# Sparse attention: an instruction order by groups of two key blocks in place of whole steps

## The reference, cut to what matters

```python
def selected_attention(q, k, v, pos, sel, slopes):      # 16 heads of 64, two key groups
    ...
        s = jnp.einsum('bghqd,bgqnld->bghqnl', qc, kg).astype(jnp.float32) * DK ** -0.5
        s = s - slopes[None, :, :, None, None, None] * dist[:, :, None]
        s = jnp.where(valid[:, :, None], s, NEG_INF).reshape(B, G, HPG, Q_BLOCK, n_top * SLC_BLOCK)
        p = jax.nn.softmax(s, axis=-1).reshape(B, G, HPG, Q_BLOCK, n_top, SLC_BLOCK).astype(v.dtype)
        return jnp.einsum('bghqnl,bgqnld->bghqd', p, vg)
...
def window_attention(q, k, v, pos, slopes):             # the same over the last 256 keys
    ...
        p = jax.nn.softmax(jnp.where(valid, s, NEG_INF), axis=-1).astype(v.dtype)
        return jnp.einsum('bghqk,bgkd->bghqd', p, vb)
...
    g = jax.nn.sigmoid(gates).reshape(B, S, 3, G, HPG).transpose(2, 0, 3, 4, 1)[..., None]
    o = g[0] * o_cmp + g[1] * o_slc + g[2] * o_win
```

## Time and profile before

| | |
|---|---|
| median of three runs | 2252.74 us |
| lowest, highest | 2248.02, 2253.5 us |
| the profiled execution: span from first to last instruction | 2245.4 us |
| the three runs less that span | 2.6 to 8.1 us, 7.3 at the median |
| mean granted TensorE clock over the span | 0.944 |
| TensorE busy in the span | 1981.3 us (88%) |
| VectorE, ScalarE, GpSimd busy | 947.7, 698.9, 456.3 us |
| sparse attention, first scores to last add | 1341.5 to 1731.5 us |
| PE busy in 1341 to 1732 | 352.87 of 391 us |

### The profile page before, as it was taken

One profiled execution on the slowest core, in us unless ns is written; L12 is line 12 of the kernel. 1 busy time (PEld: TensorE's weight loads), 2 busy tenths in 40 slices (PEclk: granted clock), 3 DMA queues, 4 the chain that ended last, 5 costly groups with the idle time before them and its releaser, 6 DMA issues. The chain is left out here.

```text
span 2245.4 us, 30273 instructions
## 1 busy us (share of the span) xinstructions
PE 1981.3 (88%) x11225; PEld 1262.1 (56%) x11225; DVE 947.7 (42%) x2302; ACT 698.9 (31%) x1761; POOL 456.3 (20%) x617
## 2 busy tenths in 40 slices
PE   6998859999969989859999768999999996999997
PEld 3444436655556756545655435666666555756664
DVE  3896874533252112114223486666664225211111
ACT  4013555531101111112122566667665110111111
POOL 0001003321022212110000255454544002122111
PEclk9999969999979999989999979999999997999999
DMA  5000010121387999863000200001001117799993
GB/s 216 0 0 0 0 47 20 39 88 66 153 362 285 383 348 377 314 210 70 1 0 1 78 1 11 11 11 48 20 11 34 77 72 316 256 379 364 353 340 119
DMA packets 80888, 307.77 MB, mean 137 GB/s; under 512 B 18352, under 2 KB 23495, under 8 KB 63846
## 3 DMA queue, kind: packets, MB, share of 16 engines
q1 hardware_dynamic: 66342, 272.23, 31.2%
q0 software_dynamic: 14400, 33.59, 5.9%
HBM read 276.75 MB, written 47.89 MB: 145 GB/s over the span
## 5 line engine op out<-in xcount | busy, mean ns | idle before, releaser
L1110 POOL TENSOR_SCALAR nsaatt_probs<-nsaatt_probs,nsaatt_inv,trunk_gates_or_logits 128x384 f32<-128x384 f32 (+7 forms) x256 | 185.6, 739 | 200.7 <-DVE nsaatt_inv L1137 200.7
L1123 DVE CUSTOM_DVE_ANT_0 nsaatt_probs<-nsaatt_scores,trunk_arena 128x384 f32<-128x384 f32 (+7 forms) x256 | 151.3, 629 | 86.3 <-PE nsaatt_scores L1029 85.7
L1834 DVE TENSOR_TENSOR experts_sig<-experts_gu_ps,experts_sig 128x256 f32<-128x256 f32 x50 | 21.2, 424 | 388.0 <-ACT experts_sig L1799 388.0
L1081 ACT ACTIVATE nsaatt_probs<-nsaatt_probs,nsaatt_bias 128x384 f32<-128x384 f32 (+7 forms) x256 | 169.0, 667 | 8.7 <-DVE nsaatt_bias L1132 8.6
L1039 PE MATMUL nsaatt_turn<-trunk_ident,nsaatt_probs 128*128 128x128 f32 x912 | 123.8, 279 | 23.4 <-POOL nsaatt_probs L1110 6.0
L1029 PE MATMUL nsaatt_scores<-layer_k_cols,trunk_x_rows 64*128 64x384 f32 (+3 forms) x640 | 128.9, 513 | 14.6 <-DVE nsaatt_top L1123 13.4
L1701 PEld LDWEIGHTS experts_gu_ps<-experts_x_cols,moew_w 128*128 128x128 f32 x1152 | 134.0, 197 | 12.1 <-issue 12.1
L1701 PE MATMUL experts_gu_ps<-experts_x_cols,moew_w 128*128 128x128 f32 x1152 | 136.7, 281 | 4.6 <-DVE experts_x_cols L1787 4.6
L1799 ACT ACTIVATE experts_sig<-experts_gu_ps 128x256 f32<-128x256 f32 x50 | 19.2, 383 | 381.0 <-PE experts_gu_ps L1701 243.6
L1039 PEld LDWEIGHTS nsaatt_turn<-trunk_ident,nsaatt_probs 128*128 128x128 f32 x912 | 97.3, 140 | 57.5 <-issue 37.6
L1713 PE MATMUL experts_gu_ps<-moew_w,experts_x_cols 128*64 128x512 f32 x256 | 97.0, 667 | 23.9 <-issue 23.9
(11 more groups left out here) (425 smaller groups left out, 3737.4 us busy)
## 6 DMA issues: line engine op xcount, KB each, us to landing
moew_w<-in_moe_w_gate_dram SPq DMA_DIRECT2D x34, 1024.0 KB, 12.4
moew_w<-in_moe_w_up_dram SPq DMA_DIRECT2D x34, 1024.0 KB, 18.2
moew_w<-in_moe_w_down_dram SPq DMA_DIRECT2D x34, 1024.0 KB, 25.6
trunk_arena<-in_moe_w_gate_dram SPq DMA_DIRECT2D x20, 1024.0 KB, 12.3
trunk_arena<-in_moe_w_up_dram SPq DMA_DIRECT2D x20, 1024.0 KB, 16.8
trunk_arena<-in_moe_w_down_dram SPq DMA_DIRECT2D x20, 1024.0 KB, 24.2
trunk_x_rows<-in_moe_w_gate_dram SPq DMA_DIRECT2D x10, 1024.0 KB, 16.3
trunk_x_rows<-in_moe_w_up_dram SPq DMA_DIRECT2D x10, 1024.0 KB, 22.3
```

The lines of the kernel that those rows point to most:

```text
L1081: act.activation(part(s, r, h), part(s, r, h), ACT.Exp, bias=bias[:, b, i:i + 1], scale=steps[s]["scale"][h], accum_out=total[:, b, i:i + ...
L1110: pool.tensor_scalar(part(s, r, h), part(s, r, h), inv[:, s % BUFS, i:i + 1], 1.0 if gate is None else gate[h], ALU.mult, ALU.mult).then_i ...
L1123: dve.tensor_tensor_reduce(part(s, r, h), scores_of(s, r, h), br["mask"], 1.0, -3e38, ALU.add, ALU.max, top[:, s % BUFS, i:i + 1]).then_in ...
```

## The change

In layer 1 (BR is 2) the loops over whole steps give way to one loop over the group number n. At position n TensorE does the values of group n-3, then the transposes of group n, then those scores that are due. The other engines run through the same positions with their own part. What is due is set by five constants: a branch's scores, masks, exponentials and inverses are placed 13, 12, 9 and 4 (window: 5) units ahead of its first group, where a group of two blocks counts 3/2.7 and one of a single block 2/2.7. The add of a step stands at the position of its last value. Layer 0's order stays, and so do all instructions, waits, tiles and buffers.

```diff
+SCORE_LAG = 13
+MASK_LAG = 12
+EXP_LAG = 9
+INV_LAG = 4
+VALUE_LAG = 3
...
+    opens = [n for n, g in enumerate(flat) if g[2] == 0]
+    weight = np.cumsum([0] + [(hi - lo + 1) / 2.7 for s, r, lo, hi in flat])
+    ENDS = range(-2 * SCORE_LAG, len(flat) + VALUE_LAG + 1)
+
+    def slot(u, lag):
+        at = weight[opens[u]] - lag
+        return int(np.floor(at)) if at < 0 else int(np.searchsorted(weight, at + 1e-9, side="right")) - 1
...
 TensorE
-                for s in range(S):
-                    if s + AHEAD < S:
-                        score(s + AHEAD, 0)
-                        if BR > 1 and not wide(s + AHEAD):
-                            score(s + AHEAD, 1)
-                    for n in range(first[s], first[s + 1]):
-                        value(n)
-                    if s + AHEAD < S and wide(s + AHEAD):
-                        score(s + AHEAD, 1)
-                    if s + 1 < S:
-                        for n in range(first[s + 1], first[s + 2]):
+                    u = 0
+                    for n in ENDS:
+                        if 0 <= n - VALUE_LAG < len(flat):
+                            value(n - VALUE_LAG)
+                        if 0 <= n < len(flat):
                             turn(n)
+                        while u < S * BR and slot(u, SCORE_LAG) <= n:
+                            score(u // BR, u % BR)
+                            u += 1
...
 ScalarE
+                    i = 0
+                    for n in ENDS:
+                        if 0 <= n < len(flat) and by_act[n]:
+                            copy_group(act, copy, n, copied_act)
+                        while i < S * SUB and slot(i // 2, EXP_LAG) + i % 2 <= n:
+                            exps(i // SUB, i % SUB // 2, i % 2)
+                            i += 1
...
 VectorE
+                    u = v = s = 0
+                    for n in ENDS:
+                        while v < S * BR and slot(v, INV_LAG + v % BR) <= n:
+                            inverse(v // BR, v % BR)
+                            v += 1
+                        if s < S and first[s + 1] - 1 + VALUE_LAG <= n:
+                            add(s)
+                            s += 1
+                        while u < S * BR and slot(u, MASK_LAG) <= n:
+                            mask(u // BR, 2 * (u % BR))
+                            mask(u // BR, 2 * (u % BR) + 1)
+                            biased(u // BR, u % BR)
+                            u += 1
+                        if 0 <= n < len(flat) and not by_act[n]:
+                            copy_group(dve, dve.tensor_copy, n, copied_dve)
```

More of the change, by code:

```diff
@@ L1055, in value @@
                     last.then_inc(valued, 1)
[L1057 to L1061, removed]
-                for s in range(S):
-                    if s + AHEAD < S:
-                        score(s + AHEAD, 0)
-                        if BR > 1 and not wide(s + AHEAD):
-                            score(s + AHEAD, 1)
-                    for n in range(first[s], first[s + 1]):
-                        value(n)
-                    if s + AHEAD < S and wide(s + AHEAD):
-                        score(s + AHEAD, 1)
-                    if s + 1 < S:
-                        for n in range(first[s + 1], first[s + 2]):
+                if BR == 1:
+                    for s in range(AHEAD):
+                        score(s, 0)
+                    for n in range(first[1]):
+                        turn(n)
+                    for s in range(S):
+                        if s + AHEAD < S:
+                            score(s + AHEAD, 0)
+                        for n in range(first[s], first[s + 1]):
+                            value(n)
+                        if s + 1 < S:
+                            for n in range(first[s + 1], first[s + 2]):
+                                turn(n)
+                else:
+                    u = 0
[3 more added lines that the diff above has]
+                        if 0 <= n < len(flat):
                             turn(n)
+                        while u < S * BR and slot(u, SCORE_LAG) <= n:
+                            score(u // BR, u % BR)
+                            u += 1
             @block.scalar
@@ L1085, in copy @@
                     return act.activation(to, source, ACT.Copy)
[L1087 to L1100, removed]
+                if BR == 1:
+                    for s in range(AHEAD - 1):
+                        exps(s, 0, 0)
+                        exps(s, 0, 1)
+                    for n in range(first[1]):
+                        if by_act[n]:
+                            copy_group(act, copy, n, copied_act)
+                    for s in range(S):
+                        if s + AHEAD - 1 < S:
+                            exps(s + AHEAD - 1, 0, 0)
+                            exps(s + AHEAD - 1, 0, 1)
+                        if s + 1 < S:
+                            for n in range(first[s + 1], first[s + 2]):
+                                if by_act[n]:
+                                    copy_group(act, copy, n, copied_act)
+                else:
+                    i = 0
+                    for n in ENDS:
+                        if 0 <= n < len(flat) and by_act[n]:
+                            copy_group(act, copy, n, copied_act)
+                        while i < S * SUB and slot(i // 2, EXP_LAG) + i % 2 <= n:
+                            exps(i // SUB, i % SUB // 2, i % 2)
+                            i += 1
             @block.gpsimd
@@ L1150, in copies @@
                             copy_group(dve, dve.tensor_copy, n, copied_dve)
[L1152 to L1167, removed]
-                            biased(s + AHEAD, 0)
[L1169 to L1181, removed]
@@ new lines, in _ @@
+                if BR == 1:
+                    for s in range(AHEAD):
+                        mask(s, 0)
+                        mask(s, 1)
+                        biased(s, 0)
+                        if s:
+                            inverse(s - 1, 0)
+                    copies(0)
+                    for s in range(S):
+                        ahead = s + AHEAD < S
+                        if ahead:
+                            mask(s + AHEAD, 0)
+                            mask(s + AHEAD, 1)
+                        add(s)
+                        if s + AHEAD - 1 < S:
+                            inverse(s + AHEAD - 1, 0)
+                        if ahead:
+                            biased(s + AHEAD, 0)
+                        if s + 1 < S:
+                            copies(s + 1)
+                else:
+                    u = v = s = 0
[4 more added lines that the diff above has]
+                        if s < S and first[s + 1] - 1 + VALUE_LAG <= n:
+                            add(s)
+                            s += 1
[6 more added lines that the diff above has]
+                            copy_group(dve, dve.tensor_copy, n, copied_dve)
```

## The result

| | before | after |
|---|---|---|
| median of 4 runs | 2252.5 us | 2279.04 us |
| lowest to highest | 2248.02 to 2253.5 | 2278.09 to 2281.22 |
| ratio of the runs, 95% interval | | 1.0131 [1.0116, 1.0147] |
| span of the profiled execution | 2245.4 us | 2276.3 us |
| sparse attention, first scores to end of last add | 389.9 us | 421.1 us |

The changed kernel is slower by 1.3%. The stage alone grew by 31.2 us (1342.96 to 1764.1 in the new trace), the span by 30.9.

What follows compares the result with a forecast made beforehand. TensorE was taken to bound the stage: 404.1 us of work, 11.5 of start waits and 8 of new waits make 423.6 against 389.9, +33.7. Span 2279.1 plus 7.3 to the median gives 2286.4 us, range 2270 to 2316.

Steps and rivals of the forecast that it cites:

- Work of the new order: TensorE in the attention stage: 444 more switches between kinds of work add 69.6 us, 404.1 us together.
- Waits that go: TensorE's waits on copies and GpSimd's scaling before transposes, most of 43 us, vanish as two positions lie between turn and value.
- Waits that come: New TensorE waits in the stage, on adds, on masks and on copies behind masks: together 8 us.
- The add's wait: Value n+1 of the next step waits for VectorE's add: 0 or 0.15 us each, about 2 us over 64 adds.
- copies behind a mask: VectorE copies queued after two wide masks end some 3.4 us after the scores, needed after 3.5; 3 us added.
- Rival B: VectorE's strictly ordered queue paces the stage: values wait 0.8 us, 32 times, 26 us on top, 2312 us; chance 14%.
- Start: Waits from the stage's first scores to its first values: 11.5 us in place of 12.3.
- The clock: Rival: TensorE's granted clock falls in the stage, a tenth of streaming at 1.2 GHz, 29 us added, 2315 us; chance 5%.
- upper case: Top of the likeliest case's own range: 93 us of switches with 20 us of waits give +70 us.
- 292 us of streaming: TensorE's streaming time in the stage, used to size the fall of the clock: a tenth at 1.2 GHz adds 29 us.

## Why the prediction was right, step by step

The direction and the mechanism were right: 2286.4 us forecast, 2279.04 measured, in the range of 2270 to 2316.

- **Work of the new order.** Forecast 404.1 us from four short stretches of the old trace. They came out as 0.59, 0.36, 0.59 and 0.37 us against 0.59, 0.36, 0.58 and 0.39. Over the whole stage their medians are 0.587, 0.369, 0.588 and 0.369. The average price was put at 0.157 us a switch; measured by itself it is 0.148.
- **Waits that go.** Idle time before transposes was to fall under 10 us; it fell from 23.4 to 0.0. All waits together fell from 55.4 to 421.1 - 404.1 = 17.0 us, where I had 19.5.
- **Waits that come.** I had 8 us for adds, masks and copies; 17.0 less 11.7 in the start leaves 5. The add's wait is there behind short transposes: 9 of 150 switches from transposes to values have a gap longer than 0.18 us, 1.4 us in all, where I had about 2. The 3 us for copies behind a mask did not come: from 1367 us on the profile lists 1.6 us of waits on masks for TensorE, and none on a copy. Rival B's 26 us did not come either: of the 64 adds in the trace none stands directly behind a mask, 58 follow an inverse and 6 a copy.
- **Start.** Forecast 11.5 us of waits. From first scores to first values 20.0 us pass, less 3,456 keys (5.8 us), some 1.3 of remainders and two stretches of transposes (1.2): 11.7. The prediction counts this work at full clock, but the granted clock in the start was 0.73, so a part of these 11.7 us is slower work and not waiting. The same holds before the change, so the difference is not touched.
- **The clock** was 1.00 on average behind 1361 us, as in the row above, and lower only in its first 6 us (0.89 in 1365 to 1367 us); before the change it had reached 1.00 by 1365.
- **The stage** was forecast at +33.7 us and grew by 31.2. The 2.5 us are the waits: 0.2 more in the start and some 3 less behind it. (The split into work and waits rests on the same prices before and after; the transposes and values can be checked start to start, the scores by their usual stretches of 0.42 and 0.85 us.)
- **The largest miss is a term that has nothing to do with the change.** I added 7.3 us for what lies between span and median. The profile of the changed kernel has 2279.04 - 2276.3 = 2.7 us there. The kernel before varies from 2246 to 2254 us between runs, its profiled execution was one of the short ones, and its first three runs had a median of 2252.74, where two sets of 19 runs beside later experiments gave 2248.91 and 2248.14. That is 4.6 of the 7.4 us by which the forecast was too high. The later runs show what belonged there: in each of them the time is 1.7 to 1.9 us above that run's own span. By this the profiled execution before took about 2247.2 us, and the other 5.5 of my 7.3 us were its distance from the median of three runs. With 1.8 in place of 7.3 the sum gives 2280.9 us.
- **The range is narrower than its own working.** Its upper case, +70 us, gives 2323 us, and the range stops at 2316. The 292 us of streaming are 294 by the prediction's terms. Neither bears on the result.

What I did not see is how near the other side lay. With 395 stretches in place of 663, the order by groups took the time of the order by steps (391.3 us, 26.5 of them waits by the same prices), and once dependent scores were kept apart it took 10 us less.

## What to carry to other kernels

Count the places where TensorE goes from one tiling to another (64-row, 64-column, full) before refining an order: each cost about 0.15 us here, and a finer interleave pays only where it removes more waiting than that. The profile books this time as busy, so compare start-to-start times of weight loads, not busy shares. The best order was a middle one, two or three groups at a time, with dependent scores kept apart by other work.

## What the runs showed of the hardware that I had not expected

- The gap does not need a wait or a change of work: a one-column matmul in another tiling, with the way back and with weights twice as wide, lengthened the stage by 0.30 us more than one in the same tiling (62.1 us over 208). The one in the same tiling lengthened it by 0.065 us (403.5 against 389.9 us, over 208), net of waits that it took up.
- Freeing TensorE gave nothing that could be measured in the order by steps: with 37 switches removed the ratio was 1.0007 [0.9993, 1.0022], while idle time before transposes grew by 3.0 us.
- The kernel before spread over 8 us from run to run and the changed one over 3. Why was not looked into.
